# All expert gates are scattered by adding writes, and the sums over equal picks are taken out

## What is computed

```python
PEER_HEADS, PEER_NKEYS, PEER_TOPK = 8, 128, 16          # 16,384 experts
q = (xc @ wq).reshape(PEER_CHUNK, PEER_HEADS, 2, PEER_HALF)
s = jnp.einsum('chpd,hpkd->chpk', q, subkeys)
s1, i1 = lax.top_k(s[:, :, 0], PEER_TOPK)
s2, i2 = lax.top_k(s[:, :, 1], PEER_TOPK)
...
cs, ci = lax.top_k(cand, PEER_TOPK)
eidx = jnp.take_along_axis(cidx, ci, axis=-1)
g = jax.nn.softmax(cs, axis=-1)
ug, vg = jnp.take(u_table, eidx, axis=0), jnp.take(v_table, eidx, axis=0)
hid = jnp.einsum('cd,chkd->chk', xc, ug)
a = jax.nn.gelu(hid, approximate=False) * g
return jnp.einsum('chk,chkd->cd', a, vg)
```

## Time and profile before

| | us |
|---|---|
| median of 3 runs | 2501.72 (2491.94 to 2502.61) |
| the profiled execution | 2497.29 |
| its span | 2495.5 |
| TensorE busy | 2294.9 (92%) |
| VectorE busy | 1299.1 (52%) |
| ScalarE busy | 901.5 (36%) |
| GpSimd busy | 1163.1 (47%) |
| adding scatters, L983, 192 | 314.8, mean 1.640 each |
| plain scatters, L980, 192 | 198.4, mean 1.034 each |

### The profile page before, as it was taken

One profiled execution on the slowest core, in us unless ns is written; L12 is line 12 of the kernel. 1 busy time (PEld: TensorE's weight loads), 2 busy tenths in 40 slices (PEclk: granted clock), 3 DMA queues, 4 the chain that ended last, 5 costly groups with the idle time before them and its releaser, 6 DMA issues.

```text
span 2495.5 us, 29790 instructions
## 1 busy us (share of the span) xinstructions
PE 2294.9 (92%) x9705; PEld 1779.3 (71%) x9712; DVE 1299.1 (52%) x2403; ACT 901.5 (36%) x1419; POOL 1163.1 (47%) x817
## 2 busy tenths in 40 slices
PE   7999999999999998975596599999999999999998
PEld 5666566787766766764385488888888788888887
DVE  4355433136323563874374366622222488888887
ACT  3554543336434443312121133322222333333333
POOL 3332121244432213375454658888820366555554
PEclk9999999999999999987697799999999999999999
DMA  6554233325321112211242167666643699999997
GB/s 211 190 191 135 70 90 103 95 87 186 114 76 60 43 35 84 70 58 39 64 139 88 55 147 147 144 145 145 135 108 108 228 330 341 355 349 358 355 357 249
DMA packets 208210, 392.32 MB, mean 157 GB/s; under 512 B 56160, under 2 KB 131936, under 8 KB 207872
## 3 DMA queue, kind: packets, MB, share of 16 engines
q1 hardware_dynamic: 151296, 323.89, 39.9%
q0 software_dynamic: 56832, 67.45, 10.8%
HBM read 330.21 MB, written 61.01 MB: 157 GB/s over the span
## 4 chain that ended last, share of the span: by engine, by line
PE 52%; issue 4%; another core or an unknown queue 3%; DVE 1%; ACT 1%; POOL 0%; DMA 0%; DVEq 0%; ACTq 0%; POOLq 0%
PE bank L1325 26%; PE bank L1336 20%; PE bank L1108 5%; PE bank L1304 1%; ACT u_tiles_split L1643 0%; POOL low L1027 0%; PE bank L1314 0%; DMA tail<-hidden_of_last_block,low 0%; DVE low L1784 0%; ACT staged L1378 0%; DVE h_low L1806 0%; DVE tail L2058 0%; DVE tail L2056 0%; DVE tail L2060 0%
## 5 line engine op out<-in xcount | busy, mean ns | idle before, releaser
L1325 PE MATMUL bank<-h_high,u_tiles_split 128*128 128x512 f32 x2048 | 643.8, 394 | 70.5 <-issue 43.9
L950 POOL TENSOR_TENSOR u_split<-blocks,u_split 128x1024 fp32r<-128x1024 f32 (+1 forms) x115 | 283.0, 2461 | 700.0 <-ACT u_split L1471 668.9
L1108 PE MATMUL bank<-h_high,u_split 128*128 128x512 f32 (+1 forms) x1712 | 567.3, 406 | 22.4 <-DVE h_low L1806 17.8
L1336 PE MATMUL bank<-v_split,a_split 128*128 128x512 f32 x2286 | 520.3, 390 | 4.6 <-DVE a_split L2096 4.6
L1325 PEld LDWEIGHTS bank<-h_high,u_tiles_split 128*128 128x128 f32 x2048 | 390.2, 191 | 162.1 <-issue 79.3
L1336 PEld LDWEIGHTS bank<-v_split,a_split 128*128 128x128 f32 x2286 | 430.1, 188 | 94.9 <-DVE v_split L2093 5.4
L1325 PE MATMUL bank<-h_low,u_tiles_split 128*128 128x512 f32 x1024 | 403.7, 394 | 14.6 <-issue 14.4
L1954 DVE TENSOR_TENSOR u_tiles_split<-tail,u_tiles_split 128x1024 fp32r<-128x1024 f32 x128 | 156.6, 1226 | 487.6 <-ACT u_tiles_split L1643 448.4
L1108 PEld LDWEIGHTS bank<-h_high,u_split 128*128 128x128 f32 (+1 forms) x1712 | 324.6, 190 | 110.9 <-issue 23.1
L983 POOL DMA_INDIRECT gates<-low x192 | 314.8, 1640 | 87.2 <-issue 58.2
L1108 PE MATMUL bank<-h_low,u_split 128*128 128x512 f32 (+1 forms) x728 | 287.9, 395 | 0.0
(11 more groups left out here) (201 smaller groups left out, 2474.9 us busy)
## 6 DMA issues: line engine op xcount, KB each, us to landing
tail<-in_uT SPq DMA_DIRECT2D x128, 512.0 KB
tail<-in_v SPq DMA_DIRECT2D x128, 512.0 KB
gates<-blocks SPq DMA_DIRECT2D x32, 768.0 KB, 5.8
tail<-gates SPq DMA_DIRECT2D x128, 192.0 KB
kept_hidden<-tail SPq DMA_DIRECT2D x96, 192.0 KB
tail<-kept_hidden SPq DMA_DIRECT2D x96, 192.0 KB
blocks<-in_r SPq DMA_DIRECT2D x24, 512.0 KB, 4.0
blocks<-in_conv SPq DMA_DIRECT2D x16, 512.0 KB, 4.2
```

The costliest lines, as they stand in the source:

```text
L950: nc.gpsimd.tensor_tensor(flat(u, 1)[:, 0:n], ring[:, loads[0] % NW, 0:n], flat(u, 0)[:, 0:n].bitcast(F32), ALU.subtract).then_inc(s_wlo, 1)
L1108: last = mm(ps[0:m, :], flat(u, part)[:, k * m:(k + 1) * m], x, start=(k == 0 and j == 0), stop=(k == nk - 1 and j == 2))
L1325: last = mm(bank[slot % 2][:, :], U4[:, slot, w, k, :], x[:, k, :], start=(k == 0 and x is hh and w == 0), stop=(k == KD - 1 and w == 1))
L1336: done = mm(bank[2 + 2 * tb + dh][:, :], A2[:, slot, wa, tb * P:(tb + 1) * P], V2[slot // 2][:, slot % 2, wv, dh * T:(dh + 1) * T], start= ...
```

## The change

All 384 scatters become adding writes. The comparison and the sums in `set_gates` go, with their tiles and the copy of the places in `retrieve`.

```diff
@@ scatter
-                if h < PLAIN:
-                    nc.gpsimd.indirect_dma_start(gate_elements, where, expert_gate[tb][:, k:k + 1], None)\
-                        .then_inc(s_sc[tb], 16)
-                else:
-                    nc.gpsimd.indirect_dma_start(gate_elements, where, expert_gate[tb][:, k:k + 1], None,
-                                                 compute_op=ALU.add).then_inc(s_sc[tb], 16)
+                nc.gpsimd.indirect_dma_start(gate_elements,
+                                             bass.IndirectOffsetOnAxis(ap=expert_no[tb][:, k:k + 1], axis=0),
+                                             expert_gate[tb][:, k:k + 1], None, compute_op=ALU.add)\
+                    .then_inc(s_sc[tb], 16)
@@ retrieve
-                if h < PLAIN:
-                    link(V.tensor_copy(earlier[:, :, ks], places))
@@ set_gates
-                if 1 <= h < PLAIN:
...
-                        link(V.tensor_tensor(same, earlier[:, tb, ks].unsqueeze(2).to_broadcast(shape),
-                                             earlier[:, tb, 0:n].unsqueeze(1).to_broadcast(shape), ALU.is_equal))
-                        link(V.tensor_tensor(same, same, expert_gate[tb][:, 0:n].unsqueeze(1).to_broadcast(shape),
-                                             ALU.mult))
-                        link(V.tensor_reduce(sum_before, same, AX.X, ALU.max))
-                        ins = V.tensor_tensor(expert_gate[tb][:, ks], expert_gate[tb][:, ks], sum_before, ALU.add)
```

More of the change, by code:

```diff
@@ L50 @@
 TD = DENSE * P
-PLAIN = 4
 LOWS_AT = (1, 2, 1, 2, 1, 2, 1, 2)
@@ L535, in program @@
         token = rt(20112, 4)
-        sum_before = rt(20116, TOPK)
-        earlier = rt(20132, DENSE * TOPK * PLAIN, DENSE)
         gf = staged[:, 0:D]
@@ L977, in scatter @@
                     pool.wait_ge(s_sc[tb], 16 * k)
-                where = bass.IndirectOffsetOnAxis(ap=expert_no[tb][:, k:k + 1], axis=0)
-                if h < PLAIN:
-                    nc.gpsimd.indirect_dma_start(gate_elements, where, expert_gate[tb][:, k:k + 1], None)\
-                        .then_inc(s_sc[tb], 16)
-                else:
-                    nc.gpsimd.indirect_dma_start(gate_elements, where, expert_gate[tb][:, k:k + 1], None,
-                                                 compute_op=ALU.add).then_inc(s_sc[tb], 16)
+                nc.gpsimd.indirect_dma_start(gate_elements,
+                                             bass.IndirectOffsetOnAxis(ap=expert_no[tb][:, k:k + 1], axis=0),
+                                             expert_gate[tb][:, k:k + 1], None, compute_op=ALU.add)\
+                    .then_inc(s_sc[tb], 16)
             scattered = 0
@@ L2033, in retrieve @@
                 link(ins)
-                places = place[:, 0:TOPK * DENSE].rearrange("p (t k) -> p t k", t=DENSE)
-                link(V.tensor_copy(expert_lists[:, 0:DENSE, ks].bitcast(U32), places))
-                if h < PLAIN:
-                    link(V.tensor_copy(earlier[:, :, ks], places))
+                link(V.tensor_copy(expert_lists[:, 0:DENSE, ks].bitcast(U32),
+                                   place[:, 0:TOPK * DENSE].rearrange("p (t k) -> p t k", t=DENSE)))
                 link(V.tensor_copy(row_no[:, ks], number[:, TOPK * DENSE:]))
@@ L2046, in set_gates @@
                 link(V.reciprocal(es[:, 4:8], es[:, 0:4]))
-                ks = slice(TOPK * h, TOPK * (h + 1))
-                ins = V.tensor_tensor(expert_lists[:, :, P + TOPK * h:P + TOPK * (h + 1)], e3,
-                                      es[:, 4:8].unsqueeze(2).to_broadcast([P, TB, 16]), ALU.mult)
-                if 1 <= h < PLAIN:
[L2051 to L2055, removed]
-                        link(V.tensor_tensor(same, earlier[:, tb, ks].unsqueeze(2).to_broadcast(shape),
-                                             earlier[:, tb, 0:n].unsqueeze(1).to_broadcast(shape), ALU.is_equal))
-                        link(V.tensor_tensor(same, same, expert_gate[tb][:, 0:n].unsqueeze(1).to_broadcast(shape),
-                                             ALU.mult))
-                        link(V.tensor_reduce(sum_before, same, AX.X, ALU.max))
-                        ins = V.tensor_tensor(expert_gate[tb][:, ks], expert_gate[tb][:, ks], sum_before, ALU.add)
-                ins.then_inc(s_tk, 1)
+                V.tensor_tensor(expert_lists[:, :, P + TOPK * h:P + TOPK * (h + 1)], e3,
+                                es[:, 4:8].unsqueeze(2).to_broadcast([P, TB, 16]), ALU.mult).then_inc(s_tk, 1)
             dve.wait_ge(s_kb[3], 16 * 4)
```

## The result

The changed kernel took **2367.29 us** (median of 4 runs, 2364.28 to 2367.88), the kernel before 2496.83 (4 runs, 2487.37 to 2502.61, three of them those of the table of before). The ratio is 0.948, with a 95% interval of 0.945 to 0.952: 5.2% faster. The prediction had been 2370. The profiled execution of the changed kernel took 2364.28 us at a span of 2362.5.

The account below looks back on a forecast made before the run. TensorE, working 92% of its span, bounds the kernel, with a hole made by plain scatters. Adding row's end 1,825.4 plus 7.8 starts the value pass at 1,833.2; plus 535.0, span 2368.2, time 2370 us; range 2345 to 2410.

Parts of the forecast that it names:

- The stalls: TensorE's hole at 1,060 to 1,430 us: four stretches of 45, 48, 32 and 43 us, made by plain scatter bursts.
- they choke whatever the other engines need from memory: How plain bursts stop TensorE, VectorE and ScalarE in the hole; what is needed was left open, no size given.
- Rival (c): Something else that coincides, such as unrolled code, makes all four stalls; time stays 2490 to 2500 us; chance 0.05.
- The scatters' pace: GpSimd's adding scatters come every 1.945 us, bounds 1.864 and 2.92; the long row of 374 ends at 1,825.4 us.
- rival (a): Row ends before 1,802.9 us, pace under 1.885 us, so the hidden pass ends last: some 2349 us; chance 0.08.
- The early pairs: Ten early scatters between weights' low parts: 1.2 to 1.4 us more per pair, long row starts 3.4 us later.
- The hidden pass: TensorE's 3,072 matmuls start at 1,113.0 and end at 1,808 us instead of 1958.1; 150 us come free.
- What is late next: Value pass waits for the row: landing 3, gate load 2.5, product to matmul 2.3; 7.8 us, start 1,833.2.
- The end: First value matmul to span end: 534.75 us, less 1.97 for a vanished pause, plus 2.2 for the clock.
- The sums: VectorE's sums in the gates, 19 us and about 1 us of copies: counted 0, at most 9 us.
- (b): Some stalls stay under adding writes: 2391 us with the first burst's 43 us, 2426 with a second; chance 0.10.
- (d): Scatter row bounds beyond the old end, slower at a pace over 2.29 us; 2,734 us at 2.92; chance 0.07.

Follow-up runs that it names:

- e5: Changed kernel with head 0's 48 scatters as plain writes: 2404.46 us, 0.958 of the kernel before, in a stalled session.
- e7: Changed kernel without the last ten picks of head 7's sixteen per dense block, 30 scatters fewer: 2346.21 us, 0.936 of the kernel before, stalled session.
- b2: The kernel before, unchanged, profiled in a second session: 2502.09 us, stalled, with the kernel before at 2499.95 beside it.
- e2: Changed kernel with plain scatters kept for heads 0 to 3, VectorE's sums out: 2346.11 us, 0.9997 of the kernel before, quiet session.
- e9: Changed kernel, head 0 plain and partly dealt out between head 1's adding scatters as in e8, four more plain ones ahead: 2345.68 us, 0.9992, quiet session.
- e1: Kernel before with all 384 scatters adding, VectorE's sums kept: 2369.19 us, 1.0099 of the kernel before, quiet session.
- e3: Kernel before with plain scatters in groups of four, each waiting until earlier groups in its block landed: 2347.99 us, 0.9999, quiet session.
- e4: Kernel before with a small GpSimd memset after every second plain scatter: 2348.55 us, 1.0008, quiet session.
- e3b: Same kernel as e3, run again on another chip: 2349.04 us, 1.0007 of the kernel before, quiet session.
- e4b: Kernel before with four small memsets behind every second plain scatter: 2345.01 us, 0.9992, quiet session.
- e4c: Same kernel as e4b, run once more: 2344.95 us, 0.9998 of the kernel before, quiet session.
- e8: Changed kernel, head 0 plain, its second and third block dealt out between head 1's adding scatters: 2354.44 us, 1.0033 of the kernel before, quiet session.

## Why the prediction was right, and where it was not

**The stalls.** The step "the hole is made by the plain bursts" held in the kind of session that the trace of before came from: the four stretches filled up, and e5 against e7 shows it with one burst. The addition "they choke whatever the other engines need from memory" did not hold: in the first stall the late thing was the signal of TensorE's matmul, 17.8 to 38.7 us behind it (b2). The sum did not use it. What I had not thought of is that the burst needs a second condition, which belongs to the session. No trace of one session could show that, and none of my rivals had it. The forecast of "faster" at 0.88 was right through the session in which it was measured; the sum of 2370 was right on its own terms. Rival (c) came closest ("something else that coincides"): the something is real, but the burst is needed too.

**The scatters' pace.** Forecast 1.945 us; measured (1819.5 - 1093.16) / 373 = 1.947. The median's 1.864 of rival (a) would have been wrong by 31 us over the row.

**The early pairs.** The step that the long row starts 3.4 us later was too large. I had put 1.2 to 1.4 us on each pair. An adding scatter behind a vector instruction took 1.57 us, so a pair is 1.57 + 0.30 + 1.55 = 3.42 us; the plain pair before, from the lines below, was 1.78 + 0.30 + 0.96 = 3.04, so 0.4 more per pair. Changed kernel, then before:

```profile
1087.14 1.57 POOL L975 DMA_INDIRECT gates<-low  x1 [0.16 <-issue]
1089.01 1.55 POOL L975 DMA_INDIRECT gates<-low  x1 [0.30 <-issue]
```
```profile
1089.26 1.78 POOL L980 DMA_INDIRECT gates<-low  x1 [0.16 <-issue]
1091.34 0.96 POOL L980 DMA_INDIRECT gates<-low  x1 [0.30 <-issue]
```

The row started at 1,093.2 and not at 1,098.3. Of the 5.1 us, 2.2 are the program before it, which was that much sooner in this execution (the key matmuls at 1,100.93 against 1,103.18), and 2.9 are this term.

**The hidden pass.** Forecast 1,113.0 to 1,808; measured 1,108.5 to 1,805.1. Its length, 695 against 696.6, held. Its start was 2.3 us sooner than the sum had it after the shift of the program; there the last two sets of key matmuls ran together (16 at once).

**What is late next.** The wait behind the row had the right sum from two wrong terms. Landing came 1.5 us after the last scatter's end (1,821.0 to 1,822.5), not 3; the gate load took 4.05 us, not 2.5 (four tiles were loaded at once and GpSimd's row gathers ran beside them; which of the two it was is not shown); product to first matmul 2.3, as forecast. Together 8.0 against 7.8, which is luck. The pause of 24 us was forecast as 25. VectorE went on at 1,842.15 (forecast 1,847), and TensorE did not stand a second time.

**The end.** 2362.5 - 1829.06 = 533.4 us against 535.0. The clock was 0.78 in the ten us from 1,830 on, (1 - 0.78) x 10 = 2.2 us, so its term held. **The sums**: 0 forecast, and e2 shows none (in a quiet session). For the heads 1 and 2 the instructions took 0.42 and 0.69 us in the trace of before, so a group was 1.4 and 2.2 us and not 1.1 and 2.1; nothing hangs on it.

**Rivals.** (a) needed a faster pace and fell. (b) fell in the first stretch. (d) fell: beside VectorE's sorting the scatters took 1.56 us at the median. By the rule of the Trainium skill (SBUF — State Buffer, section SBUF: two separate sides) a VectorE copy in a two-port mode beside them would have lengthened them; with VectorE busy 32.99 of 48 us in the second stretch, this trace shows none of it either.

## What to carry to other kernels

A hole in the busiest engine may be the doing of another engine's transfers. Look which engine alone goes on through it, and compare a stretch with the other kind of transfer in the same trace. Then measure again in another session before a gain of 5% is booked: here it was that in one kind of session, and in the other a kernel with the same scatters lost 1%. Look also whether the traces of the two sessions hold the same number of records. And a step that gets dearer off the critical path has a last moment by which it must end; here one sum, 374 times the pace, told that the row would end 17 us past the pass that hides it and TensorE stand for 25, and dealing the cheap writes of one head into it (e9) took that back in a quiet session.

## What the runs showed of the hardware that I had not expected

- Single-element plain scatters from GpSimd, 128 elements every 1.26 us, stopped TensorE, VectorE and ScalarE in two of six sessions, from about 10 to 40 us after a burst began. In the other four they stopped nobody (e2 by its trace, with 1.36 us at the mean; the kernel before by its time). Ordinary loads had the same time to landing in both kinds (256 KB 2.7 us, 512 KB of weights 3.5 to 3.6), outside the bursts.
- During the first stall the DMA engines were 2% busy. In b2, in 30 us of its first stall, GpSimd's queue moved 768 packets for 24 scatters, as many per scatter as in quiet times: the writes went out at the pace of their issue, and the others still stood. What came late were the signals of TensorE's matmuls (17.8 and 38.7 us) and of VectorE.
- Adding scatters of the same size, one per 1.95 us, began no stall in either kind of session: 384 in the changed kernel and 354 in e7 in the stalled ones, 384 in e1 in a quiet one. In e5 a stall that plain ones had begun went on for 18 us under them. Whether it is their kind or their pace stays open: e3, e4, e3b, e4b, e4c, e8 and e9 were made for it and all ran in quiet sessions. What the session's condition is stays open too; the loss of signal records goes with it in all 14 traces.
